# Expert matrices loaded as two halves with a semaphore each, and one transposed tile taken by ScalarE

## The chip, the core and the metric

The program runs on one core of one Trainium2 chip. Such a core has a matrix engine (TensorE, PE in the profile), a vector engine (DVE), an activation engine (ScalarE, ACT), GpSimd (POOL), a queue engine that issues transfers (SyncE, SP), and 16 DMA engines that share each transfer. The metric is the time of one execution on the device, in microseconds (us). A transfer is told to be complete by a semaphore that an engine waits on.

## The reference, cut to what matters

One layer over 256 tokens of width 1024, in float32. Three branches (chunked attention, a Mamba-2 scan, attention into a memory) are merged and added to x; then comes a mixture of experts, which the change is about:

```python
logits = (xt @ w_router + b_router)
top_val, top_idx = lax.top_k(logits, 4)          # 4 of 32 experts for each token
wts = softmax(top_val)
# for each expert e, its tokens' rows xblk:
g = xblk @ w_gate[e] + b_gate[e]                 # 1024 x 1024, float32: 4 MB
u = xblk @ w_up[e] + b_up[e]                     # 4 MB
g, u = min(g, 7.0), clip(u, -7.0, 7.0)
yb = ((u + 1) * g * sigmoid(1.702 * g)) @ w_down[e] + b_down[e]    # 4 MB
# weighted sum of yb over each token's experts, added to x
```

All 32 experts are computed, so 96 matrices of 4 MB are read from HBM.

## The kernel before, in words

The first part (up to about 520 us) streams the other weights through four buffers and computes the branches and the output projection. Its last block is the second column block of `w_out` (block "wo", 1), computed for two tiles of 128 tokens. For each tile t VectorE adds the product to x (`add_out`), TensorE turns (transposes) the upper four column chunks of the tile (`turn_out`), VectorE copies the turned columns out of PSUM into `xT` (`take_xT`, L1433), and TensorE finishes the router's logits from them (`last_logits`, L1618 is the router's matmul). Beside it ScalarE squares the tile with an accumulated sum (L899), VectorE scales the sum (`norm_begin`, L1439), ScalarE takes a root (L694), VectorE makes the inverse root and the top-4 choice (`choose`), and ScalarE writes the normed tile `h2` (L905).

The second part works through the 32 experts in order. For each expert TensorE does, in this order: the gate matmuls (`gate_or_up`, L1954), the scatter of the expert before (L1935), the up matmuls (L1954), the gather for the next expert (L1878) around the transposes of the activation, and the down matmuls (`down`, L1992). Each of the three matrices takes 8 chunks of 128 rows, two matmuls of 512 columns each; between chunk 3 and 4 of gate and up stand two matmuls of the bias (L1962).

The matrices are numbered m = 3e + k (k is 0 for gate, 1 for up, 2 for down) and go round five slots of 4 MB in the on-chip memory (slot m % 5). The SP queue issues the load of matrix m when matrix m - 5 is done with (semaphores `gate_done`, `up_done`, `down_done`). The loads of SP run in the order of issue. The first five matrices come in pieces during the first part. The loads m = 5 to 9 go out in two halves of 2 MB (chunks 0 to 3, then 4 to 7): the first half when TensorE has done the first half of matrix m - 5 (`half_done`), the second when it has done all of it. From m = 10 to 92 (83 matrices) one load brings the whole matrix in 32 KB runs, one for each of 128 partitions (L610), and TensorE waits for all of it before its first chunk. The last three matrices go out as two halves one behind the other, when the slot is free, with a semaphore for each half.

The experts 0 and 1 stand before TensorE's loop, 2 to 26 in a loop of five rounds of five, 27 to 31 behind it; SP's loop covers the loads m = 10 to 84.

Of the kernel before, what the change touches and what calls it, by code (L numbers as in the profile page):

```python
# [249 lines left out]
def hybrid_block_kernel(nc, x, mem, g_mix, w_in, w_dt, a_gains, rel_rev, conv_w, conv_b, dt_bias, a_log, d_skip,  # L250
                        g_ssm, g_mem, w_mem_kv, x_gains, w_br_a, w_br_b, w_br_c, w_out, norm_ffn, w_router,
                        b_router, w_gate, b_gate, w_up, b_up, w_down, b_down, bias_dram, out):
    with ExitStack() as ctx:
# [186 lines left out]
        MATRICES = EXPERTS * LOADS  # L440
        ROUND, ROUNDS = 5, 5
        AHEAD, TURNS = 2, ROUND * LOADS // SLOTS
        HALVED = MATRICES - LOADS
        FIRST_PIECES = (2, 2, 4, 4, 3)
        e_landed = [sem(f"expert_landed{k}") for k in range(SLOTS)]
        e_done = [sem("gate_done"), sem("up_done"), sem("down_done")]
        half_landed = [[sem(f"last_landed{k}{h}") for h in range(2)] for k in range(LOADS)]

        def landings(slot, turn):

            return 16 * (FIRST_PIECES[slot] + (turn and turn + 1))

        MISC_END = MISC_AT["end"]
        COUNT_BANK = EXP_BANK
# [48 lines left out]
        def _(sp):  # L503
# [8 lines left out]
                sp.dma_start(halves[:, m % HALVES], weight_src(name, i)[:, 4 * (m % 2):4 * (m % 2) + 4])\  # L512
                    .then_inc(landed[m % HALVES], 16)

            def matrix_load(m, c0=0, c1=KC, signal=None):

                slot, chunks = m % SLOTS, slice(c0, c1)
                sp.dma_start(eslots[slot][:, chunks], expert_src(m % LOADS, m // LOADS)[:, chunks])\
                    .then_inc(signal or e_landed[slot], 16)

            def bias_loads():

# [72 lines left out]
            sp.wait_ge(sem("x_opened"), 2 * TT)  # L595
            matrix_load(4, 6, 8)

            for m in range(SLOTS, 2 * SLOTS):
                freed = m - SLOTS
                sp.wait_ge(sem("half_done"), freed + 1)  # L600
                matrix_load(m, 0, 4)
                sp.wait_ge(e_done[freed % LOADS], freed // LOADS + 1)
                matrix_load(m, 4, 8)

            def round_loads(j, n0, n1):

                for n in range(n0, n1):
                    m, freed = 2 * SLOTS + n, SLOTS + n
                    sp.wait_ge(e_done[freed % LOADS], j * ROUND + freed // LOADS + 1)
                    sp.dma_start(eslots[m % SLOTS], expert_src(m % LOADS, j * ROUND + m // LOADS))\  # L610
                        .then_inc(e_landed[m % SLOTS], 16)

            with sp.Fori(0, ROUNDS) as j:
                round_loads(j, 0, ROUND * LOADS)
            round_loads(ROUNDS, 0, HALVED - 2 * SLOTS - ROUNDS * ROUND * LOADS)
            for k in range(LOADS):
                m = HALVED + k
                sp.wait_ge(e_done[(m - SLOTS) % LOADS], (m - SLOTS) // LOADS + 1)
                for half in range(2):
                    matrix_load(m, 4 * half, 4 * half + 4, half_landed[k][half])  # L620

            sp.wait_ge(sem("passes_known"), 1)
            n_pass = sp.value_load(npass_i[0:1, 0:1], min_val=1, max_val=PASSES)
            with sp.If(n_pass > 1):
                with sp.Fori(1, n_pass) as b:
                    with sp.Fori(0, EXPERTS) as e:
                        for k in range(LOADS):

                            sp.wait_ge(sem("down_done"), b * EXPERTS + e)
                            sp.dma_start(eslots[k], expert_src(k, e)).then_inc(half_landed[k][0], 16)  # L630
            for t in range(TT):
                sp.wait_ge(sem("y_ready"), t + 1)
                sp.dma_start(out[0, t * P:(t + 1) * P, 0:NB], y_out[:, 2 * t]).then_inc(sem("y_stored"), 16)
# [54 lines left out]
        def _(act):  # L688
# [207 lines left out]
            for t in range(TT):  # L896
                act.wait_ge(gemm_taken, GEMM_AT[("wo", 1, t)] + 1)
                act.wait_ge(sem("out_squares"), TT + t)
                act.activation(tmp[:, t], x_sb[:, t, NB:2 * NB], ACT.Square, accum_out=ss_part[:, TT + t:TT + t + 1])\  # L899
                    .then_inc(sem("out_squares"), 1)  # L900
                root(1)
                act.wait_ge(sem("second_norm"), t + 1)
                for h in range(2):
                    cols = slice(h * NB, (h + 1) * NB)
                    act.activation(h2[:, t].rearrange("q (c p) -> q c p", c=KC)[:, :, 64 * h:64 * h + 64],  # L905
                                   x_sb[:, t, cols].rearrange("q (p c) -> q c p", c=KC), ACT.Copy, scale=rs_2[:, t:t + 1]).then_inc(sem("h2_ready"), 1)
# [29 lines left out]
        def _(dve):  # L936
# [493 lines left out]
            def take_xT(t):  # L1430
# [2 lines left out]
                dve.tensor_copy(xT[:, 4:8, t * P:(t + 1) * P], ps[:, b, :].rearrange("p (c t) -> p c t", c=4))\  # L1433
                    .then_inc(misc_taken, 1)

            def norm_begin(t):

                dve.wait_ge(sem("out_squares"), TT + t + 1)
                link(dve.tensor_tensor(ss_2[:, t:t + 1], ss_part[:, t:t + 1], ss_part[:, TT + t:TT + t + 1], ALU.add))  # L1439
                variance(rs_2[:, t:t + 1], ss_2[:, t:t + 1], D)  # L1440
# [47 lines left out]
                dve.tensor_copy(pick[0:96], picks[0:96, column(i)].to_broadcast([96, BLK])).then_inc(sem("pick_ready"), 1)  # L1488

            add_out(0)  # L1490
            take_xT(0)
            norm_begin(0)
            choose(0)
            add_out(1)
            take_xT(1)
            norm_begin(1)
            find_first(0)
            choose(1)
            dve.tensor_tensor(e4, mx8[:, :, 0:TOP_K], mx8[:, :, 0:1].to_broadcast([P, TT, TOP_K]), ALU.subtract)\
# [81 lines left out]
        def _(pe):  # L1581
# [362 lines left out]
            pe.wait_ge(sem("logits_taken"), TT)  # L1944
            pe.wait_ge(sem("passes_known"), 1)
            n_pass = pe.value_load(npass_i[0:1, 0:1], min_val=1, max_val=PASSES)
            def gate_or_up(i, k, pieces, halves_done=False):

                bank = (G_BANK, U_BANK)[k]
                for slot, c0, c1, landed_at, count in pieces:  # L1950
                    pe.wait_ge(landed_at, count)
                    for c in range(c0, c1):
                        for h in range(2):
                            last = pe.matmul(ps[64 * h:64 * h + 64, bank, :].rearrange("j (m q) -> j m q", q=4),  # L1954
                                             xgT[:, c], hidden_of(eslots[slot][:, c], h),
                                             start=c == 0, stop=c == KC - 1, skip_group_check=True)
                        if c == KC // 2 - 1:
                            if halves_done:
                                last.then_inc(sem("half_done"), 1)
                            pe.wait_ge(sem("pick_ready"), i + 1)  # L1960
                            for h in range(2):
                                pe.matmul(ps[64 * h:64 * h + 64, bank, :].rearrange("j (m q) -> j m q", q=4),  # L1962
                                          pick[0:96], hidden_of(bias_parts[0:96, k], h),
                                          start=False, stop=False, skip_group_check=True)
                last.then_inc(e_done[k], 1)
# [12 lines left out]
                    last = turn(ps[:, G_BANK, c * P:(c + 1) * P], act_sb[:, c * P:(c + 1) * P])  # L1978
                last.then_inc(sem("actT_out"), 1)

            def down(i, pieces, halves_done=False):

                pe.wait_ge(sem("actT_ready"), i + 1)
                pe.wait_ge(sem("scatter_ready"), i + 1)
# [3 lines left out]
                for slot, c0, c1, landed_at, count in pieces:  # L1988
                    pe.wait_ge(landed_at, count)
                    for c in range(c0, c1):  # L1990
                        for h in range(2):
                            last = pe.matmul(ps[64 * h:64 * h + 64, D_BANK, :], actT[:, c % 4, 64 * (c // 4):64 * (c // 4) + 64],  # L1992
                                             eslots[slot][:, c, h * NB:(h + 1) * NB],
                                             start=False, stop=c == KC - 1, skip_group_check=True)
                        if halves_done and c == KC // 2 - 1:
                            last.then_inc(sem("half_done"), 1)
                last.then_inc(e_done[2], 1)

# [3 lines left out]
                    pe.matmul(ps[:, X_BANK, c % KC * BLK:(c % KC + 1) * BLK], h2[:, 0, c % KC * P:(c % KC + 1) * P],  # L2002
                              hot[:, 0], start=True, stop=True, skip_group_check=True)

            def expert(i, loads, ahead=True, halves_done=(False, False, False)):

                pe.wait_ge(sem("xg_ready"), i + 1)
                gate_or_up(i, 0, loads[0], halves_done[0])
                scatter(i)
                turn_places(i)  # L2010
                gate_or_up(i, 1, loads[1], halves_done[1])
                if ahead:
                    pe.wait_ge(sem("hot_ready"), i * TT + 2 * TT)
                    gather(0, 1)
# [2 lines left out]
                else:  # L2017
                    keep_warm(KC)
                    turn_activation(i)
                    keep_warm(KC // 2)  # L2020
                down(i, loads[2], halves_done[2])

            def whole(m, j=0):

                slot, turn = m % SLOTS, m // SLOTS
                return [(slot, 0, KC, e_landed[slot], landings(slot, turn) + 16 * TURNS * j)]

            for e in range(AHEAD):
                expert(e, [whole(LOADS * e + k) for k in range(LOADS)],
                       halves_done=[LOADS * e + k < SLOTS for k in range(LOADS)])  # L2030
            with pe.Fori(0, ROUNDS) as j:
                for r in range(ROUND):
                    e = AHEAD + r
                    expert(j * ROUND + e, [whole(LOADS * e + k, j) for k in range(LOADS)])
            for e in range(AHEAD + ROUNDS * ROUND, EXPERTS - 1):
                expert(e, [whole(LOADS * e + k) for k in range(LOADS)])
            expert(EXPERTS - 1, [[((HALVED + k) % SLOTS, 4 * half, 4 * half + 4, half_landed[k][half], 16)
                                  for half in range(2)] for k in range(LOADS)], ahead=False)

            with pe.If(n_pass > 1):  # L2040
                with pe.Fori(1, n_pass) as b:
                    with pe.Fori(0, EXPERTS) as e:
                        i = b * EXPERTS + e
                        pe.wait_ge(sem("hot_ready"), i * TT + TT)
                        gather()
                        expert(i, [[(k, 0, KC, half_landed[k][0], ((b - 1) * EXPERTS + e + 2) * 16)] for k in range(LOADS)],
                               ahead=False)
            scatter(n_pass * EXPERTS, sem("sums_ready"))

# [39 lines left out]
```

## Time and profile before

| | us |
|---|---|
| median of 3 runs | 1448.0 (1447.46 to 1449.2) |
| the profiled execution | 1448.57 |
| its span, first to last instruction | 1446.5 |
| TensorE busy | 1425.7 (99%) |
| VectorE busy | 589.0 (41%) |
| ScalarE busy | 407.0 (28%) |

The granted clock of TensorE is 0.999 over the span. The page says that matmuls are pipelined and that their ends are modelled, so a high busy share is no proof that no other limit is near: the chain of waits and the DMA rows have to be read with it. The time between an issue of a transfer and its landing holds the waiting behind the transfers ahead of it in the queue.

### The profile page before, as it was taken

Reading aid. Unit: us, or ns where it says so; the run is one execution under the profiler, and the core shown is the slowest. Engines: PE = TensorE matmul, PEld = TensorE weight load, DVE = VectorE, ACT = ScalarE, POOL = GpSimd, SP = SyncE. Lnnn points to the kernel's source line nnn. Section 1 sums busy time; section 2 is a strip of 40 time slices with the busy share of each in tenths; the row PEclk is TensorE's granted clock in tenths of the full one; section 3 lists DMA queues with packets and bytes.
Section 4 is the critical chain, followed back from the end, with each engine's and each line's share of the span. In section 5 each row is a group of like instructions: output and inputs, shape, how many; then the busy total and the mean of one; then the engine's idle time right before and its main releaser. Section 6 shows DMA issues by size and latency. Waiting matters only on the chain.

```text
span 1446.5 us, 18510 instructions
## 1 busy us (share of the span) xinstructions
PE 1425.7 (99%) x7576; PEld 823.3 (57%) x7576; DVE 589.0 (41%) x1154; ACT 407.0 (28%) x605; POOL 63.9 (4%) x50
## 2 busy tenths in 40 slices
PE   7999999999999999999999999999999999999998
PEld 6998888777788864444444444444444444444433
DVE  6789788677788651211212121121212112111211
ACT  5766666556544531101010110101011010101100
POOL 5110000121100000000000000000000000000000
PEclk9999999999999999999999999999999999999999
DMA  7455544655563989999999999999999999999996
GB/s 237 157 190 173 162 136 160 197 162 164 171 244 139 382 328 420 406 432 434 433 425 433 433 435 431 426 435 433 434 428 430 433 435 432 428 432 433 432 424 255
DMA packets 62646, 490.84 MB, mean 339 GB/s; under 512 B 4009, under 2 KB 7729, under 8 KB 48001
## 3 DMA queue, kind: packets, MB, share of 16 engines
q1 hardware_dynamic: 59920, 487.04, 82.9%
q10 hardware_dynamic: 2160, 2.62, 0.6%
q8 instruction: 38, 0.62, 0.2%
q0 software_dynamic: 512, 0.43, 0.2%
q14 instruction: 16, 0.12, 0.0%
HBM read 488.41 MB, written 1.07 MB: 338 GB/s over the span
## 4 chain that ended last, share of the span: by engine, by line
PE 88%; DMA 6%; DVE 4%; ACT 1%; issue 1%; ACTq 0%; SPq 0%; DVEq 0%
PE ps L1954 29%; PE ps L1992 13%; PE ps L1611 8%; PE ps L1613 8%; PE ps L1612 8%; PE ps L1878 7%; DMA regions<-in_w_gate 6%; PE ps L1935 4%; PE ps L1598 4%; DVE regions L1187 1%; DVE splits L1041 1%; PE ps L1832 1%; PE ps L1962 1%; PE ps L1986 1%; ACT splits L726 0%
## 5 line engine op out<-in xcount | busy, mean ns | idle before, releaser
L1954 PE MATMUL ps<-regions,sig 128*64 128x512 f32 x2048 | 463.0, 594 | 3.8 <-DMA regions<-in_w_gate 3.6
L1954 PEld LDWEIGHTS ps<-regions,sig 128*64 128x64 f32 x2048 | 143.8, 137 | 274.1 <-issue 266.8
L1992 PE MATMUL ps<-regions,tmp 128*64 128x512 f32 x1024 | 225.1, 592 | 0.0
L1611 PE MATMUL ps<-splits,regions_r 128*128 128x512 f32 x512 | 205.7, 402 | 0.1
L1613 PE MATMUL ps<-splits,regions_r 128*128 128x512 f32 x512 | 200.1, 391 | 0.0
L1612 PE MATMUL ps<-splits,regions_r 128*128 128x512 f32 x512 | 199.8, 390 | 0.0
L726 ACT ACTIVATE splits<-halves 128x1024 fp32r<-128x1024 f32 x152 | 159.2, 1056 | 93.4 <-PE ps L1613 82.1
L1041 DVE TENSOR_TENSOR splits<-halves,splits 128x1024 fp32r<-128x1024 f32 x132 | 162.2, 1232 | 42.9 <-ACT splits L726 41.5
L914 ACT ACTIVATE work<-work 128x512 f32<-128x512 f32 x32 | 20.1, 629 | 473.9 <-DVE work L1545 473.9
L1992 PEld LDWEIGHTS ps<-regions,tmp 128*64 128x64 f32 x1024 | 71.5, 137 | 132.2 <-issue 129.8
L1878 PEld LDWEIGHTS ps<-craw,regions 128*128 128x128 f32 x1024 | 119.3, 192 | 25.6 <-issue 25.1
L1878 PE MATMUL ps<-craw,regions 128*128 128x64 f32 x1024 | 124.7, 275 | 0.4 <-DVE craw L1466 0.4
L1550 DVE TENSOR_SCALAR work<-ps 128x512 f32<-128x512 f32 x32 | 22.1, 691 | 238.8 <-PE ps L1954 238.8
L1611 PEld LDWEIGHTS ps<-splits,regions_r 128*128 128x128 f32 x512 | 96.2, 188 | 22.4 <-issue 3.9
L1559 DVE COPY sig<-ps 128x512 f32<-128x512 f32 x32 | 22.1, 691 | 211.1 <-PE ps L1992 211.1
L1613 PEld LDWEIGHTS ps<-splits,regions_r 128*128 128x128 f32 x512 | 96.1, 188 | 20.9
L1612 PEld LDWEIGHTS ps<-splits,regions_r 128*128 128x128 f32 x512 | 96.3, 188 | 18.6
L919 ACT ACTIVATE tmp<-ps 128x512 f32<-128x512 f32 x32 | 19.1, 597 | 302.1 <-PE ps L1598 302.1
L1545 DVE TENSOR_SCALAR work<-ps 128x512 f32<-128x512 f32 x32 | 22.1, 692 | 177.0 <-PE ps L1954 177.0
L1935 PE MATMUL ps<-sig,craw 64*128 64x512 f32 x264 | 65.6, 615 | 0.8 <-DVE sig L1559 0.8
L681 POOL TENSOR_TENSOR splits<-halves,splits 128x1024 fp32r<-128x1024 f32 x20 | 49.8, 2491 | 327.9 <-ACT splits L726 327.9
L1611 PE MATMUL ps<-regions_r,splits 128*128 128x256 f32 x192 | 55.5, 289 | 0.0
(304 smaller groups left out, 1192.2 us busy)
## 6 DMA issues: line engine op xcount, KB each, us to landing
regions<-in_w_up SPq DMA_DIRECT2D x28, 4096.0 KB, 27.2
regions<-in_w_down SPq DMA_DIRECT2D x28, 4096.0 KB, 29.8
regions<-in_w_gate SPq DMA_DIRECT2D x27, 4096.0 KB, 29.4
halves<-in_w_in SPq DMA_DIRECT2D x48, 1024.0 KB, 5.1
regions<-in_w_gate SPq DMA_DIRECT2D x8, 2048.0 KB, 11.4
regions<-in_w_up SPq DMA_DIRECT2D x7, 2048.0 KB, 11.9
regions<-in_w_down SPq DMA_DIRECT2D x6, 2048.0 KB, 12.3
halves<-in_w_br_b SPq DMA_DIRECT2D x8, 1024.0 KB, 5.1
```

Source lines behind the costliest of these rows:

```text
L681: pool.tensor_tensor(lo, raw, hi.bitcast(F32), ALU.subtract).then_inc(lo_ready_pool, 1)
L726: act.activation(hi, raw, ACT.Copy).then_inc(hi_ready, 1)
L1041: dve.tensor_tensor(lo, raw, hi.bitcast(F32), ALU.subtract).then_inc(lo_ready, 1)
L1545: dve.tensor_scalar(g_sb, ps[:, G_BANK, :], LIMIT, None, ALU.min).then_inc(sem("g_ready"), 1)
L1598: return pe.transpose(dst, src, ident[:])
L1611: pe.matmul(out, lhs[0], rhs[0], start=start, stop=False, skip_group_check=True)
L1612: pe.matmul(out, lhs[1], rhs[0], start=False, stop=False, skip_group_check=True)
L1613: return pe.matmul(out, lhs[0], rhs[1], start=False, stop=stop, skip_group_check=True)
L1878: last = pe.matmul(ps[:, X_BANK, c * BLK:(c + 1) * BLK], h2[:, t, c * P:(c + 1) * P], hot[:, t], start=(t == 0 and c == 0), stop=(t == TT ...
L1935: last = pe.matmul(ps[:, ACC[2 * t + h], :], hot_wT[rows, t], yb[rows], start=False, stop=False, skip_group_check=True)
L1954: last = pe.matmul(ps[64 * h:64 * h + 64, bank, :].rearrange("j (m q) -> j m q", q=4), xgT[:, c], hidden_of(eslots[slot][:, c], h), start= ...
L1992: last = pe.matmul(ps[64 * h:64 * h + 64, D_BANK, :], actT[:, c % 4, 64 * (c // 4):64 * (c // 4) + 64], eslots[slot][:, c, h * NB:(h + 1) ...
```

## The change

Three things change in the code. First, every load from m = 5 on goes out as two halves of 2 MB in 16 KB runs, the first half when the first half of matrix m - 5 is done with, the second when all of it is; this is now so inside SP's loop too, which therefore starts at m = 5. Second, each slot has two semaphores, one for each half, and TensorE waits for a half ahead of that half's chunks, in every matrix; it signals `half_done` in every matrix. Third, the turned columns of the second tile are copied out of PSUM by ScalarE, right behind its squares, and VectorE waits at that place for it (`left_to_scalar`); on VectorE `norm_begin(0)` now stands ahead of `take_xT(0)`.

```diff
-        FIRST_PIECES = (2, 2, 4, 4, 3)
-        e_landed = [sem(f"expert_landed{k}") for k in range(SLOTS)]
+        FIRST_PIECES = ((1, 1), (1, 1), (2, 2), (2, 2), (1, 2))
+        e_landed = [[sem(f"expert_landed{k}{h}") for h in range(2)] for k in range(SLOTS)]
...
-            for m in range(SLOTS, 2 * SLOTS):
+            def reload(m, j=0):
+
                 freed = m - SLOTS
-                sp.wait_ge(sem("half_done"), freed + 1)
-                matrix_load(m, 0, 4)
-                sp.wait_ge(e_done[freed % LOADS], freed // LOADS + 1)
-                matrix_load(m, 4, 8)
-
-            def round_loads(j, n0, n1):
-
-                for n in range(n0, n1):
-                    m, freed = 2 * SLOTS + n, SLOTS + n
-                    sp.wait_ge(e_done[freed % LOADS], j * ROUND + freed // LOADS + 1)
-                    sp.dma_start(eslots[m % SLOTS], expert_src(m % LOADS, j * ROUND + m // LOADS))\
-                        .then_inc(e_landed[m % SLOTS], 16)
+                sp.wait_ge(sem("half_done"), j * ROUND * LOADS + freed + 1)
+                matrix_load(m, 0, 4, j * ROUND)
+                sp.wait_ge(e_done[freed % LOADS], j * ROUND + freed // LOADS + 1)
+                matrix_load(m, 4, 8, j * ROUND)
 
             with sp.Fori(0, ROUNDS) as j:
-                round_loads(j, 0, ROUND * LOADS)
-            round_loads(ROUNDS, 0, HALVED - 2 * SLOTS - ROUNDS * ROUND * LOADS)
-            for k in range(LOADS):
-                m = HALVED + k
-                sp.wait_ge(e_done[(m - SLOTS) % LOADS], (m - SLOTS) // LOADS + 1)
-                for half in range(2):
-                    matrix_load(m, 4 * half, 4 * half + 4, half_landed[k][half])
+                for m in range(SLOTS, SLOTS + ROUND * LOADS):
+                    reload(m, j)
+            for m in range(SLOTS + ROUNDS * ROUND * LOADS, MATRICES):
+                reload(m)
...
+                if t == 1:
+                    n_misc = MISC_AT["tail"] + t
+                    act.wait_ge(misc_ready, n_misc + 1)
+                    act.activation(xT[:, 4:8, t * P:(t + 1) * P],
+                                   ps[:, MISC_BANKS[n_misc % 3], :].rearrange("p (c t) -> p c t", c=4), ACT.Copy)\
+                        .then_inc(misc_taken, 1)
...
             add_out(0)
+            norm_begin(0)
             take_xT(0)
-            norm_begin(0)
             choose(0)
             add_out(1)
-            take_xT(1)
             norm_begin(1)
+            left_to_scalar()
...
-                            if halves_done:
-                                last.then_inc(sem("half_done"), 1)
+                            last.then_inc(sem("half_done"), 1)
...
-            def whole(m, j=0):
+            def in_halves(m, j=0):
 
                 slot, turn = m % SLOTS, m // SLOTS
-                return [(slot, 0, KC, e_landed[slot], landings(slot, turn) + 16 * TURNS * j)]
+                return [(slot, 4 * half, 4 * half + 4, e_landed[slot][half], landings(slot, half, turn) + 16 * TURNS * j)
+                        for half in range(2)]
```

On SP's queue, where the reloads of the slots end their straight part and enter the loop, there stood before the halves of m = 8 and 9, the loop's head and its first whole loads (128 partitions of 8192 elements are a whole matrix, 4096 are a half):

```order
44 L518 DMA regions<-in_w_down 128x4096 x2
45 L518 DMA regions<-in_w_gate 128x4096 x2
46 L613 UNCONDITIONAL_BRANCH
47 L613 ISA
48 L610 ISA
49 L610 DMA regions<-in_w_up 128x8192
50 L610 DMA regions<-in_w_down 128x8192
```

At the end of the loop and behind it there stands now, on the same queue:

```order
89 L517 DMA regions<-in_w_up 128x4096 x2
90 L605 REGISTER_ALU
91 L605 COMPARE_AND_BRANCH
92 L517 DMA regions<-in_w_down 128x4096 x2
93 L517 DMA regions<-in_w_gate 128x4096 x2
94 L517 DMA regions<-in_w_up 128x4096 x2
```

Every whole load has become two halves; the order of the matrices is as it was.

On VectorE, at the second tile of the last output block, there stood before (`regions<-ps 128x4x128` is the copy of the turned columns):

```order
585 L1427 TENSOR_TENSOR regions<-regions,ps 128x512
586 L1433 COPY regions<-ps 128x4x128
587 L1439 TENSOR_TENSOR stat<-stat 128x1
588 L957 TENSOR_SCALAR stat<-stat 128x1
589 L1464 TENSOR_TENSOR rt<-ps,chosen_r 128x32
```

On ScalarE the same stretch now reads (the squares of the second tile, then the copy, the root, and the two halves of `h2`):

```order
292 L888 ACTIVATE tmp,stat<-regions 128x512
293 L893 ACTIVATE regions<-ps 128x4x128
294 L683 ACTIVATE stat<-stat 128x1
295 L900 ACTIVATE regions<-regions,stat 128x8x64 x2
```

The copy of the second tile has moved from VectorE to ScalarE, ahead of the root.

## Rows read from the trace of the kernel before

**Rows 1.** The page: span, TensorE's busy time, DMA share in 40 slices.

```profile
span 1446.5 us, 18510 instructions
PE 1425.7 (99%) x7576; PEld 823.3 (57%) x7576; DVE 589.0 (41%) x1154; ACT 407.0 (28%) x605; POOL 63.9 (4%) x50
DMA  7455544655563989999999999999999999999996
```

**Rows 2.** Waits of TensorE: in total us, times, longest us.

```profile
PE ps L1954 <- DMA regions<-in_w_gate: 3.6, 3, 2.2
```

**Rows 3.** Chain that ended last: start us, us, what; expert 1.

```profile
563.03 3.43 PE ps L1954 x16
...
584.30 6.87 PE ps L1992 x32
591.17 3.43 PE ps L1954 x16
```

**Rows 4.** The same chain, from the loop's end to the last expert's end.

```profile
1283.20 40.54 DMA regions<-in_w_gate
...
1340.85 42.65 DMA regions<-in_w_gate
1383.50 0.14 issue
1383.63 3.65 PE ps L1954 x16
...
1412.07 3.43 PE ps L1954 x16
...
1428.71 1.93 PE ps L2002 x16
...
1432.45 6.90 PE ps L1992 x32
```

**Rows 5.** DMA queue: packets, MB, share of 16 engines; 1000:1300, then 1403:1427.

```profile
q1 hardware_dynamic: 4449, 129.53, 100.3%
...
q1 hardware_dynamic: 708, 10.29, 100.8%
```

**Rows 6.** Timeline of SP's queue: start us, us, instruction; five issues.

```profile
563.07 0.33 SPq L518 DMA_DIRECT2D regions<-in_w_up  x1
...
579.70 0.33 SPq L518 DMA_DIRECT2D regions<-in_w_gate  x1
...
692.40 0.33 SPq L610 DMA_DIRECT2D regions<-in_w_gate  x1
...
1369.98 0.80 SPq L518 DMA_DIRECT2D regions<-in_w_gate  x2
...
1390.99 0.80 SPq L518 DMA_DIRECT2D regions<-in_w_down  x2
```

**Rows 7.** First load of each of rows 6: KB, us from issue to landing.

```profile
regions<-in_w_up SPq DMA_DIRECT2D x1, 2048.0 KB, 10.2
...
regions<-in_w_gate SPq DMA_DIRECT2D x1, 2048.0 KB, 13.2
...
regions<-in_w_gate SPq DMA_DIRECT2D x1, 4096.0 KB, 19.3
...
regions<-in_w_gate SPq DMA_DIRECT2D x1, 2048.0 KB, 37.8
...
regions<-in_w_down SPq DMA_DIRECT2D x1, 2048.0 KB, 36.4
```

**Rows 8.** Timeline around the second tile's copy, with idle time and releaser.

```profile
525.76 0.63 ACT L899 ACTIVATE tmp<-regions 128x512 f32<-128x512 f32 x1 [1.45 <-DVE regions L1427]
...
526.30 0.19 ACT L899 ACTIVATION_READ_ACCUMULATOR tmp<-regions 128x1 f32 x1
...
526.37 1.10 PE L1885 MATMUL ps<-regions,ident 128*128 128x512 f32 x2
526.54 0.69 DVE L1433 COPY regions<-ps 128x512 f32<-128x512 f32 x1 [0.81 <-PE ps L1905]
...
527.31 0.50 PE L1618 MATMUL ps<-wr_sb,regions 128*128 128x32 f32 x3
```

**Rows 9.** The page's groups: a ScalarE copy of 512 columns out of PSUM.

```profile
L919 ACT ACTIVATE tmp<-ps 128x512 f32<-128x512 f32 x32 | 19.1, 597 | 302.1 <-PE ps L1598 302.1
```

More of the change, by code:

```diff
@@ L442, in hybrid_block_kernel, with landings @@
         AHEAD, TURNS = 2, ROUND * LOADS // SLOTS
-        HALVED = MATRICES - LOADS
-        FIRST_PIECES = (2, 2, 4, 4, 3)
-        e_landed = [sem(f"expert_landed{k}") for k in range(SLOTS)]
+        FIRST_PIECES = ((1, 1), (1, 1), (2, 2), (2, 2), (1, 2))
+        e_landed = [[sem(f"expert_landed{k}{h}") for h in range(2)] for k in range(SLOTS)]
         e_done = [sem("gate_done"), sem("up_done"), sem("down_done")]
-        half_landed = [[sem(f"last_landed{k}{h}") for h in range(2)] for k in range(LOADS)]
-        def landings(slot, turn):
-            return 16 * (FIRST_PIECES[slot] + (turn and turn + 1))
+        again_landed = [sem(f"again_landed{k}") for k in range(LOADS)]
+        def landings(slot, half, turn):
+            return 16 * (FIRST_PIECES[slot][half] + turn)
         MISC_END = MISC_AT["end"]
@@ L513, in load, with matrix_load @@
                     .then_inc(landed[m % HALVES], 16)
-            def matrix_load(m, c0=0, c1=KC, signal=None):
+            def matrix_load(m, c0, c1, before=0):
                 slot, chunks = m % SLOTS, slice(c0, c1)
-                sp.dma_start(eslots[slot][:, chunks], expert_src(m % LOADS, m // LOADS)[:, chunks])\
-                    .then_inc(signal or e_landed[slot], 16)
+                sp.dma_start(eslots[slot][:, chunks], expert_src(m % LOADS, before + m // LOADS)[:, chunks])\
+                    .then_inc(e_landed[slot][c0 // 4], 16)
             def bias_loads():
@@ L629, in _ @@
                             sp.wait_ge(sem("down_done"), b * EXPERTS + e)
-                            sp.dma_start(eslots[k], expert_src(k, e)).then_inc(half_landed[k][0], 16)
+                            sp.dma_start(eslots[k], expert_src(k, e)).then_inc(again_landed[k], 16)
             for t in range(TT):
@@ L1434, in take_xT, with left_to_scalar @@
                     .then_inc(misc_taken, 1)
+            def left_to_scalar():
+                misc[0] += 1
+                dve.wait_ge(misc_taken, misc[0])
             def norm_begin(t):
@@ L1946, in _, with gate_or_up @@
             n_pass = pe.value_load(npass_i[0:1, 0:1], min_val=1, max_val=PASSES)
-            def gate_or_up(i, k, pieces, halves_done=False):
+            def gate_or_up(i, k, pieces):
                 bank = (G_BANK, U_BANK)[k]
@@ L1979, in turn_activation, with down @@
                 last.then_inc(sem("actT_out"), 1)
-            def down(i, pieces, halves_done=False):
+            def down(i, pieces):
                 pe.wait_ge(sem("actT_ready"), i + 1)
@@ L1994, in down @@
                                              start=False, stop=c == KC - 1, skip_group_check=True)
-                        if halves_done and c == KC // 2 - 1:
+                        if c == KC // 2 - 1:
                             last.then_inc(sem("half_done"), 1)
@@ L2003, in keep_warm, with expert @@
                               hot[:, 0], start=True, stop=True, skip_group_check=True)
-            def expert(i, loads, ahead=True, halves_done=(False, False, False)):
+            def expert(i, loads, ahead=True):
                 pe.wait_ge(sem("xg_ready"), i + 1)
-                gate_or_up(i, 0, loads[0], halves_done[0])
+                gate_or_up(i, 0, loads[0])
                 scatter(i)
                 turn_places(i)
-                gate_or_up(i, 1, loads[1], halves_done[1])
+                gate_or_up(i, 1, loads[1])
                 if ahead:
@@ L2020, in expert @@
                     keep_warm(KC // 2)
-                down(i, loads[2], halves_done[2])
-            def whole(m, j=0):
+                down(i, loads[2])
+            def in_halves(m, j=0):
                 slot, turn = m % SLOTS, m // SLOTS
-                return [(slot, 0, KC, e_landed[slot], landings(slot, turn) + 16 * TURNS * j)]
+                return [(slot, 4 * half, 4 * half + 4, e_landed[slot][half], landings(slot, half, turn) + 16 * TURNS * j)
+                        for half in range(2)]
             for e in range(AHEAD):
-                expert(e, [whole(LOADS * e + k) for k in range(LOADS)],
-                       halves_done=[LOADS * e + k < SLOTS for k in range(LOADS)])
+                expert(e, [in_halves(LOADS * e + k) for k in range(LOADS)])
             with pe.Fori(0, ROUNDS) as j:
@@ L2033, in _ @@
                     e = AHEAD + r
[L2034 to L2038, printed above, removed]
+                    expert(j * ROUND + e, [in_halves(LOADS * e + k, j) for k in range(LOADS)])
+            for e in range(AHEAD + ROUNDS * ROUND, EXPERTS):
+                expert(e, [in_halves(LOADS * e + k) for k in range(LOADS)], ahead=e < EXPERTS - 1)
             with pe.If(n_pass > 1):
@@ L2045, in _ @@
                         gather()
-                        expert(i, [[(k, 0, KC, half_landed[k][0], ((b - 1) * EXPERTS + e + 2) * 16)] for k in range(LOADS)],
+                        expert(i, [[(k, 0, KC, again_landed[k], ((b - 1) * EXPERTS + e + 1) * 16)] for k in range(LOADS)],
                                ahead=False)
```

## The prediction, made before the changed kernel ran

> **What bounds the kernel now.** I read the page's busy shares and 40 slices first. TensorE is busy 99% of the span, and from the sixteenth slice on the DMA engines are at nine tenths or more as well [rows 1]. Two resources are thus near their limit in the expert stage, and the page alone doesn't say which one ends it. The waits of TensorE name only 3.6 us in three waits, all for a gate matrix [rows 2]. The chain of waits shows how the two compare: in expert 1 it is TensorE alone, 591.17 - 563.03 = 28.14 us for three matrices [rows 3]. Late in the stage it runs over two DMA pieces, of 40.54 and 42.65 us from issue to landing, and TensorE starts 0.14 us after the second has landed [rows 4]. In the middle of the stage such a load took 19.3 us [rows 6, 7]. So the time to landing grows while TensorE goes on undisturbed: the DMA engines are a little slower than TensorE and use up a lead.
>
> Their rate comes from landings a known number of matrices apart. The gate load issued at 692.40 landed at 711.70 [rows 6, 7], the one issued at 1283.20 at 1323.74 [rows 4]; 21 experts, 63 matrices, lie between them, so a whole matrix takes 612.04 / 63 = 9.715 us, 29.14 for an expert against TensorE's 28.14. That is 1.0 us of lead lost in each expert. The lead is gone near the end of the loop; from there the DMA engines set the pace. From 1323.74 to the landing at 1383.50 (1340.85 + 42.65) six matrices took 59.76 us where 6 x 9.715 = 58.3 were due: 1.5 us were lost once, just behind the place where the loops end [rows 4]. The cause isn't in these rows.
>
> **The change, part by part.** *Loads in halves.* What a free slot half gives is an earlier issue, and what a landed half gives is an earlier start. The second counts only where TensorE waits, the first only where the DMA engines would run dry. They are busy 100.3% of the time from 1000 to 1300 [rows 5], and a load lands 19.3 us after its issue at 692 and 40.5 at 1283 [rows 4, 6, 7], so loads are always queued and an earlier issue moves nothing through them faster. The number of bytes is the same. What is left is the price of a transfer in halves.
>
> That price can be read, because the kernel before has halves in two places. Second halves of m = 7 and 9, issued at 563.07 and 579.70, landed at 573.27 and 592.90: two matrices in 19.63 us, 9.815 each. First halves of m = 93 and 95, issued at 1369.98 and 1390.99, landed at 1407.78 and 1427.39: 19.61, 9.805 each [rows 6, 7]. The places are far apart, one with 10 us of loads queued and one with 37, and agree. I take 9.81, and a matrix in halves costs 9.81 - 9.715 = 0.095 us more. The rounding of the landings (0.1 us) leaves 0.05 to 0.14. A second reading goes by the busy time of the engines for each MB: 1.003 x 300 / 129.53 = 2.323 us from 1000 to 1300, all in whole matrices, and 1.008 x 24 / 10.29 = 2.351 from 1403 to 1427, all in halves [rows 5]: 1.2%, or 0.118 us for 4.19 MB. So 83 matrices change from whole to halves at 0.05 to 0.14 us: 4 to 12 us of DMA time, 8 by my value.
>
> *The sum.* The DMA queue is full from the load that lands at 592.90 on: the first half of m = 10 now goes out near 584.30 + 3.43 = 587.7 [rows 3], before that landing. The second half of the last up matrix, m = 94, is 85 matrices later: 592.90 + 85 x 9.81 = 1426.75. Behind it TensorE has, from rows of the last experts, 0.14 to start [rows 4], 3.65 for the second half of up, as in the half-matrix behind a wait [rows 4], 1432.45 - 1428.71 = 3.74 for the turned activation and bias, and 6.90 for down: 14.43, an end at 1441.18. The other chain through the last expert (its gate's first half lands three halves earlier, then gate, scatter and up without a pause) comes to the same within 0.1. The last down half lands two halves, 9.81 us, after m = 94 and has 0.8 us to spare for its own 3.4 us of matmuls.
>
> To this I add the 1.5 us lost behind the loops. Both loops end at nearly the same place in both programs and with the same kind of code behind them, so I take it to come again: 1442.7. Before, the last down matmul ended at 1432.45 + 6.90 = 1439.35 [rows 4]. The difference is +3.3 us.
>
> Check of the wait that goes: the 3.6 us of waits [rows 2] are what the DMA pace costs before. They don't vanish, they grow, and are spread over halves: small waits at the gate's first and second half of each expert, from about expert 26 on, some 1.2 us for each.
>
> *Signals and waits on TensorE.* Some 90 more signals and as many more waits. Expert 1 has its gate and up signalled by halves and took 28.14 us [rows 3]; in the last expert, whose matrices are waited for by halves, half a gate takes 3.43 us at 1412.07 as it does at 591.17 in the loop [rows 3, 4]. I take 0. From above, 90 waits at the 0.14 us that a start takes behind a wait would be 12 us, but that is paid only where the semaphore isn't there yet. From below it is 0, since nothing is removed.
>
> *SP's queue.* Twice the issues at 0.33 us [rows 6], 6 for an expert of 28 us, with nothing behind them but loads in the same order. A half waits for TensorE's own half, so the queue never stands in its own way. 0.
>
> *The second tile's copy.* VectorE copied the turned columns at 526.54 in 0.69 us, and TensorE's router matmuls, which need them, start at 527.31; TensorE is still in the matmuls of L1885 until 526.37 + 1.10 = 527.47 [rows 8]. ScalarE has done with its squares at 526.30 + 0.19 = 526.49 [rows 8], so it is free at the same moment, and such a copy takes it 0.60 us [rows 9]. So the router starts within 0.1 us of where it did. What VectorE wins (0.69 us off its queue) falls in a stretch where TensorE works on without a wait for it. If ScalarE's copy comes late by d, the router's matmuls come late by d less 0.1: I bound it by -0.2 and +0.3 and take 0. `norm_begin(0)` ahead of the first copy puts two small instructions into time in which VectorE waits for the turned columns: 0.
>
> The sum is +3.3 us. The profiled execution took 1448.57 us, 2.1 over its span and 0.6 over the median of 1448.0. From the median: 1448.0 + 3.3 = 1451.3.
>
> **A rule that speaks against it.** The landings above say that a matrix in two transfers costs 0.095 us more [rows 6, 7]. The Trainium skill, page "DMA: Bandwidth & Descriptors", section "Anatomy of one DMA", says that on trn2 the semaphore write's bubble is about one cycle, essentially free, and its "Rules for kernel authors" ask only for 1 MiB per transfer, which halves of 2 MB meet. By that rule splitting is free, and the first rival below would be the outcome.
>
> **The rivals.** *A: halves cost nothing, faster.* If the two places with halves are slow for a reason of their own (both stand in straight code outside the loops, not in the stretch where whole loads were timed), the rate stays 9.715. Then m = 94 lands at 592.90 + 85 x 9.715 = 1418.7, with the 1.5 us 1420.2, and the end by the same 14.43 is 1434.6. TensorE alone, 30 periods of 28.14 from 563.03 and then the 27.28 us that the last expert takes (1439.35 - 1412.07 [rows 4]), gives 1434.5. So -4.8 us, 1443.2. It decides from a price below 0.055 us for a matrix, where the end is the old one; at 0.04 the end would be 1438.0. For it speaks that no row shows halves inside the loop; against it, that two places 830 us apart agree to 0.01 us, and that the busy time for each MB says the same.
>
> *B: the 1.5 us don't come again.* The sum is then +1.8 us, 1449.8. For it speaks that it is seen once only. Against it, that it follows the loops' end, which stays.
>
> *C: halves are dearer, or a second such loss comes.* At 0.118 us for a matrix, by the busy time, the sum gains 85 x 0.023 = 2.0 us: +5.3, 1453.3. A second loss of 1.5 us gives 1452.8.
>
> *D: the change isn't felt.* If TensorE alone set the pace, nothing but the 3.6 us of waits could change. The growth from 19 to 42 us to landing speaks against it.
>
> **How the numbers follow.** About 0.2%, 2.9 us, is what can be told from no change here. Forecast (+3.3): 0.45; B: 0.2; C: 0.15; A: 0.2. Of the forecast a third of its weight lies below 2.9 us by the rounding of the price, say 0.1 of 0.45. Slower: 0.35 + 0.15 = 0.50. Same: 0.10 + 0.20 = 0.30. Faster: 0.20, all of A. The range takes in B and C with the upper end of the copy's bound, and of A the part with a small price: 1444.0 to 1453.5. The forecast's own range is 1449.5 to 1453.
>
> **What would show it.** Landings of matrices one expert apart in the loop: 29.4 us, not 29.1. DMA packets of 16 KB throughout, and a busy time of 2.35 us for each MB. Time to landing of a half near 40 us at the end, and waits of TensorE for gate (and a little for up) of 6 to 9 us in total, from about expert 26 on. No change of the 28.14 us of an expert before that, and the first matmul of expert 0 within 0.3 us of where it was. I am wrong if the loop shows 29.14 us for three matrices in halves (A), or if an expert takes TensorE more than 28.2 us without a wait for DMA.

## The result, and the profile after

| | median us | runs |
|---|---|---|
| before | 1448.13 (1447.3 to 1449.95) | 22 |
| changed | 1450.11 (1448.86 to 1451.31) | 22 |

The ratio is 1.0013, with a 95% interval of 1.0007 to 1.0019: the change makes the kernel 2.0 us slower. The profiled execution has a span of 1448.1 us against 1446.5, 1.6 more, so the difference can be followed in the two traces. The page after, in the lines that answer to [rows 1]:

```profile
span 1448.1 us, 18768 instructions
PE 1426.6 (99%) x7576; PEld 821.8 (57%) x7576; DVE 588.6 (41%) x1153; ACT 407.5 (28%) x606; POOL 63.9 (4%) x50
DMA  7455545655464989999999999999999999999996
```

At this grain nothing has moved. The waits of TensorE have (in total us, times, longest), against [rows 2]:

```profile
PE ps L1954 <- DMA regions<-in_w_gate: 4.2, 6, 0.9
...
PE ps L1954 <- DMA regions<-in_w_up: 0.4, 1, 0.4
```

There are more of them and each is shorter: before, three waits with one of 2.2 us, now seven of at most 0.9. They begin earlier too. The chain that ended last (start us, us, what) goes over its first DMA piece one expert sooner than in [rows 4], and then over one for every second expert:

```profile
1254.50 43.37 DMA regions<-in_w_gate
...
1311.39 46.41 DMA regions<-in_w_gate
...
1371.33 45.56 DMA regions<-in_w_gate
...
1426.71 3.65 PE ps L1954 x16
1430.37 1.93 PE ps L2001 x16
...
1434.11 6.90 PE ps L1991 x32
```

The last rows are the ones that the forecast's sum was built of: the second half of the last up matrix, the turning of the activation, and down. TensorE's last down matmul ends at 1434.11 + 6.90 = 1441.01, against 1439.35 before.

The price of halves inside the loop can now be read. In SP's timeline (start us, us, instruction) a second half of a gate matrix goes out at 691.96, and its row of DMA issues says 18.6 us to landing:

```profile
691.96 0.33 SPq L517 DMA_DIRECT2D regions<-in_w_gate  x1
```

```profile
regions<-in_w_gate SPq DMA_DIRECT2D x1, 2048.0 KB, 18.6
```

It landed at 710.56, and the one issued at 1254.50 at 1297.87. They are 20 experts apart: 587.31 / 60 = 9.79 us for a matrix, against 9.715 before. The DMA queue's row (packets, MB, share of 16 engines) from 1000 to 1300, which answers to the first of [rows 5], says the same: 128.54 MB where before 129.53 went through, 0.76% less.

```profile
q1 hardware_dynamic: 8821, 128.54, 100.6%
```

The packets have doubled (4449 before). The second tile's copy, against [rows 8]:

```profile
525.91 0.18 ACT L888 ACTIVATION_READ_ACCUMULATOR tmp<-regions 128x1 f32 x1
525.98 1.10 PE L1885 MATMUL ps<-regions,ident 128*128 128x512 f32 x2
...
526.15 0.60 ACT L893 ACTIVATE regions<-ps 128x512 f32<-128x512 f32 x1
...
526.92 0.97 PE L1618 MATMUL ps<-wr_sb,regions 128*128 128x32 f32 x8
```

The router's matmuls start 526.92 - 525.98 = 0.94 us behind L1885, before 527.31 - 526.37 = 0.94. ScalarE's copy is done at 526.75 and TensorE doesn't feel the difference.

### The profile page after: what moved, and what is told of

Read it like the earlier page. It is cut to its first block, busy times and chain, and to the rows that moved or that the text cites. A ratio compares the mean times of both kernels' runs of the same rounds, so it can differ in the third digit from the quotient of the medians.

```text
span 1448.1 us, 18768 instructions
## 1 busy us (share of the span) xinstructions
PE 1426.6 (99%) x7576; PEld 821.8 (57%) x7576; DVE 588.6 (41%) x1153; ACT 407.5 (28%) x606; POOL 63.9 (4%) x50
## 3 DMA queue, kind: packets, MB, share of 16 engines
HBM read 488.41 MB, written 1.07 MB: 338 GB/s over the span
## 4 chain that ended last, share of the span: by engine, by line
PE 84%; DMA 10%; DVE 4%; ACT 1%; issue 1%; ACTq 0%; DVEq 0%
PE ps L1954 27%; PE ps L1991 12%; DMA regions<-in_w_gate 9%; PE ps L1611 8%; PE ps L1613 8%; PE ps L1612 8%; PE ps L1878 7%; PE ps L1935 4%; PE ps L1598 4%; DVE regions L1182 1%; DVE splits L1036 1%; PE ps L1832 1%; PE ps L1961 1%; PE ps L1985 1%; ACT splits L715 0%
```

## The experiments

Times are medians, with the ratio to the kernel before, run on the same chip, and its 95% interval. "Lost time" below is how much longer the landings took from the first half of m = 7 to the last up half, m = 94, than 9.715 us for each whole matrix and 4.895 for each half make.

**Which part carries the difference: `copy_only` and `halves_only`.** The first is the kernel before with the ScalarE and VectorE edits alone:

```diff
+                if t == 1:
+                    act.wait_ge(misc_ready, n_misc + 1)
+                    act.activation(xT[:, 4:8, t * P:(t + 1) * P], ...).then_inc(misc_taken, 1)
...
-            take_xT(1)
+            left_to_scalar()
```

> The kernel before with only the second tile's copy on ScalarE and norm_begin(0) ahead of the first copy; the loads are as before. My theory: nothing on the path, 0.0 to -0.2 us against before (from the traces, 9.73 us from the first open_sum to expert 0's first matmul before, 9.63 in the changed kernel). Rival (ScalarE's copy comes late and holds the router's matmuls): slower by 0.3 us or more.

Measured: 1448.00 against 1448.03, ratio 0.9997 (0.9988 to 1.0006). The second is the changed kernel without those edits.

> The changed kernel with the second tile's copy and norm_begin put back on VectorE as before; all loads in halves. My theory: the loads carry the whole difference, +1.5 to +2.3 us against before, landings of halves 4.895 us apart in the loop. Rival (the copy's move costs and the halves do not): within 0.5 us of before.

Measured: 1450.29, ratio 1.0016 (1.0007 to 1.0025), +2.3 us. The loads carry the whole difference.

**What is dear in a half: `one_load_short_runs` and `quarters`.** Halves differ from whole loads in two ways: twice the transfers with a completion each, and runs of 16 KB instead of 32. The first kernel changes the runs alone:

```diff
-                    sp.dma_start(eslots[m % SLOTS], expert_src(m % LOADS, j * ROUND + m // LOADS))\
+                    sp.dma_start(halves_swapped(eslots[m % SLOTS]),
+                                 expert_src(m % LOADS, j * ROUND + m // LOADS).rearrange("p (h c) n -> p h (c n)", h=2))\
```

> The kernel before, but each whole load in the loops is still one transfer with one completion, now in 16 KB runs instead of 32 KB (the first and second 16 KB of each partition land in swapped places, so that the products pair wrong rows; the work is the same). Theory R (the price is one for each run): landings 9.79 us apart, last landing 83 x 0.075 = 6.2 us later, time +3.5 to +4.5 us. Theory P (the price is one for each transfer and its completion): landings 9.715 us apart as before, time within 0.3 us of before.

Measured: 1454.40, ratio 1.0041 (1.0026 to 1.0057). The landings in the loop are 9.79 us apart (the slope over 58 landings), just as in the changed kernel, with one transfer for each matrix. So the price is one for the shorter runs, and a second transfer with its completion costs nothing that these traces show. The time is 6.4 us longer and not the 3.5 to 4.5 expected: TensorE here waits for whole matrices at the lower rate. The last DMA piece of its chain is a whole up matrix of the last expert but one, which lands at 1399.97, and TensorE works on from there without a wait to its last down matmul:

```profile
1358.62 41.35 DMA regions<-in_w_up
```

The second kernel cuts each half once more:

```diff
+                for c in range(c0, c1, 2):
+                    chunks = slice(c, c + 2)
+                    sp.dma_start(eslots[slot][:, chunks], ...).then_inc(e_landed[slot][c0 // 4], 16)
```

> The changed kernel with each half load split once more, into two transfers of 1 MB in 8 KB runs; waits and places in the order as in the changed kernel. If the price is a constant for each further piece (0.075 us for the second), four pieces cost 3 x 0.075 = 0.225 us: 9.94 us for a matrix, last landing 85 x 0.15 = 12.8 us later than in the changed kernel, time +14 to +15 us against before. Rival (the DMA engines have the same rate for any piece of 1 MB or more, and the 9.79 us of the changed kernel have another cause such as the issue in halves): the time of the changed kernel, +2 us.

Measured: 1463.65, ratio 1.0113 (1.0098 to 1.0129), +16.1 us, 1.1 above the expected range; the last up piece lands 13.1 us later than in the changed kernel, where 12.8 were expected. The queue's rows from 1000 to 1200 of this kernel, then of `one_load_short_runs`, then of the changed one:

```profile
q1 hardware_dynamic: 11587, 84.37, 101.3%
```

```profile
q1 hardware_dynamic: 5552, 85.66, 100.6%
```

```profile
q1 hardware_dynamic: 5888, 85.72, 100.7%
```

4.194 MB x 200 / 84.37 = 9.94 us for a matrix in quarters, as expected, and 9.79 for both others. The last two rows also show the completions apart from the runs: for a matrix `one_load_short_runs` has 5552 x 4.194 / 85.66 = 272 packets (256 runs and 16 more), the changed kernel 288 (256 and 32), at the same rate. Each of the 16 engines moves 8 runs of a whole matrix, 16 of one in 16 KB runs, 32 of one in 8 KB runs: (9.79 - 9.715) / 8 and (9.94 - 9.715) / 24 are both 9 ns for each run more.

**A cut by partitions: `two_loads_long_runs`.**

```diff
+                    for q in range(2):
+                        lanes = slice(64 * q, 64 * q + 64)
+                        sp.dma_start(eslots[m % SLOTS][lanes], expert_src(...)[lanes])\
+                            .then_inc(e_landed[m % SLOTS], 16)
```

> The kernel before, but each whole load in the loops goes out as two transfers of 64 partitions each, in 32 KB runs, TensorE still waits for both. Theory P (a price for each transfer): two transfers 9.79 us for a matrix, time +3.5 to +4.5 us. Theory R (a price for each run): 9.715 us for a matrix and the time of before within 0.3 us. If 64 partitions at a time use the engines or ports unevenly, both are wrong and the matrix takes clearly over 9.8 us.

Measured: 2299.87, ratio 1.5892 (1.5868 to 1.5916). Both theories' numbers are missed, and the reserve that the expectation named holds, far more than "clearly". Its queue from 1000 to 1200:

```profile
q1 hardware_dynamic: 1602, 42.01, 100.2%
```

The engines are as busy as ever and move 210 GB/s, half of the usual rate. Why 64 partitions at a time are so slow is not shown here. So this kernel doesn't tell a price for a transfer from one for a run; `one_load_short_runs` does.

**What the start by halves is worth: `wait_for_both`.** The changed kernel with both waits ahead of the first chunk:

```diff
-                for slot, c0, c1, landed_at, count in pieces:
-                    pe.wait_ge(landed_at, count)
+                for piece in pieces:
+                    pe.wait_ge(*piece[3:5])
+                for slot, c0, c1, landed_at, count in pieces:
```

> The changed kernel, but TensorE waits for both halves ahead of the first chunk of each matrix; loads, their order and issue as in the changed kernel. My theory: the same landings; the start by halves is worth half a matrix at the last waits, 3.6 us: time +5 to +6 us against before. Rival (the DMA pace alone sets the end, and the start by halves is worth nothing): +2 us as the changed kernel.

Measured: 1453.88, ratio 1.0043 (1.0028 to 1.0058), +6.4 us, 4.4 more than the changed kernel and 0.4 above the expected range. The end of its chain:

```profile
1387.01 40.01 DMA regions<-in_w_up
1427.02 0.14 issue
1427.16 3.65 PE ps L1955 x16
...
1431.04 3.44 PE ps L1955 x16
```

The last up half lands at 1427.02, within 0.4 us of where it does in the changed kernel (1426.64 by its issue and time to landing), and now all of the up matrix stands behind it, not half. The halves' semaphores are thus worth half a matrix and a little: with the shorter runs and waits for whole matrices the kernel is 6.4 us slower, the waits by halves give back 4.4, and 2.0 are left. That `one_load_short_runs` comes to 6.4 as well is partly luck: there the last up half lands 2.3 us later (1429.36), but the last expert is still waited for by halves.

**Halves only where TensorE waits: `late_halves` and `mostly_whole`.** The first is the kernel before with halves from m = 85 on instead of 93; of its edit, the line that sets this:

```diff
-        HALVED = MATRICES - LOADS
+        HALVED = 2 * SLOTS + ROUNDS * ROUND * LOADS
```

> The kernel before with whole loads up to m = 84 and halves with a semaphore each from m = 85 (before: from m = 93); issue of both halves when the slot is free. My theory: 8 matrices more at 0.075 us cost 0.6 us, the start by halves gives back the waits for whole loads: the end is set by the landing of the last up half, 14.4 us ahead of it, 1437.6 against 1439.4 before: -1.5 to -2 us. Rival (halves cost their price and give nothing): +0.6 us.

Measured: 1445.73 against 1447.52, ratio 0.9987 (0.9978 to 0.9997), -1.8 us. The end of the chain:

```profile
1368.18 43.96 DMA regions<-in_w_gate
...
1421.98 3.65 PE ps L1953 x16
...
1429.38 6.90 PE ps L1991 x32
```

The last down matmul ends at 1436.28. Landings are at the pace of before, and the end follows the last up half as in the changed kernel.

The second adds an early issue for m = 10 and the move of the copy; of its edit, the lines for m = 10:

```diff
-            for m in range(SLOTS, 2 * SLOTS):
+            for m in range(SLOTS, EARLY):            # EARLY = 2 * SLOTS + 1
```

> As late_halves, with m = 10 too in halves with an early issue, the loop of whole loads over m = 11 to 85, halves from m = 86, and the second tile's copy on ScalarE. My theory: the DMA engines no longer run dry at about 592 us (2.2 us in the trace of before), so the landings come 2 us earlier: 592.9 + 9.79 + 75 x 9.715 + 9 x 9.79 + 1.5 = 1420.9, + 14.4 = 1435.3 against 1439.35: -3.5 to -4.5 us against before, and TensorE alone is nearly the limit. Rival (the gap at 592 us is made up for by nothing, since the loss has another cause): -1.5 to -2 us as late_halves.

Measured: 1445.29, ratio 0.9981 (0.9972 to 0.9990), -2.2 us. This beats both the kernel before and the changed one; from `late_halves` it can't be told, since the two intervals overlap. My theory of it is wrong by half. The gap near 592 us did go: the load of m = 11 lands at 597.24 + 14.5 = 611.74, before at 598.32 + 16.2 = 614.52. But of the 2.3 us lost there before, only 1.0 us stands at m = 10, where the queue ran short; 1.3 us stand at m = 11. And in `mostly_whole` landings are 0.6, 1.5 and 1.4 us late at 631.8, 662.3 and 1412.4 us, so that the lost time is 3.6 us in this kernel as in the one before (2.9 in `late_halves`). The rival's number held. What the late landings are is the next question.

**What the lost time is: `straight_15` and `straight_25`.** A landing that is late by 1.35 us stands behind the loops in the changed kernel as well (the rows of issue at 1294.13 and 1297.57, landings 42.9 and 45.7 us later). Around it the DMA queue's rows (1340 to 1342) show a packet of instructions:

```profile
q1 hardware_dynamic: 56, 0.79, 92.3%
q8 instruction: 1, 0.02, 3.4%
```

In the traces of the kernel before and of the changed one such packets come until about 726 us, the end of the loop's first round, and again from 1312 on. To test the link I gave the same work more code outside the loops:

```diff
-        ROUND, ROUNDS = 5, 5
+        ROUND, ROUNDS = 5, 3        # straight_25: 5, 1
```

> The changed kernel with three rounds of the loops instead of five: experts 17 to 31 stand as straight code behind the loop (15 instead of 5), the work and its order are the same. Theory F (the landings lost behind the loops come from fetching instructions, since the 16 KB packets of the instruction queue stop at about 726 us and start again at 1312 us in the traces): these packets now begin near 1030 us, some 11 more of them ahead of the last landings, and the lost time, 3.4 us in the changed kernel from the landing of m = 7 to that of m = 94, grows by 2 to 4 us; time +2 to +4 us against the changed kernel, so +4 to +6 against before. Rival (the losses have nothing to do with the code): the time of the changed kernel, +2 us against before.

> The changed kernel with one round of the loops: experts 7 to 31 stand as straight code. Theory F: some 22 more instruction packets than in the changed kernel, from about 730 us on without a pause, lost time up by 4 to 8 us, time +6 to +10 us against before. Rival: +2 us as the changed kernel, and no growth from 15 to 25 straight experts.

Measured: 1451.65, ratio 1.0028 (1.0017 to 1.0040), and 1454.15, ratio 1.0044 (1.0027 to 1.0061): +3.6 and +6.1 us. The instruction queue's row from 568 to 1420 in the changed kernel, in `straight_15` and in `straight_25`:

```profile
q8 instruction: 12, 0.20, 0.1%
```

```profile
q8 instruction: 23, 0.38, 0.2%
```

```profile
q8 instruction: 35, 0.57, 0.3%
```

The time grows with the packets: both medians lie above the changed kernel's, by 1.6 and 4.1 us, though `straight_15` is just below the +4 us expected and its interval touches the changed kernel's. The lost time is 3.4, 4.3 and 6.0 us, a growth of 0.9 and 2.6 where 2 to 4 and 4 to 8 were expected. One trace of each is a weak measure of it: among the kernels with the changed kernel's packets it goes from 1.7 us (`wait_for_both`) to 4.2 (`one_load_short_runs`). Only `straight_25` stands clear of that.

Stronger evidence lies in where the late landings are. In `straight_25` they come at every eighth packet, and add up to the whole lost time (all in us):

| packet starts | next late landing | late by | next packet starts | next late landing | late by |
|---|---|---|---|---|---|
| 699.6 | 705.3 | 0.46 | 726.4 | 730.8 | 1.07 |
| 895.2 | 897.8 | 0.45 | 922.6 | 928.2 | 1.09 |
| 1091.2 | 1095.1 | 0.46 | 1112.5 | 1115.7 | 1.04 |
| 1286.1 | 1292.4 | 0.46 | 1311.6 | 1317.9 | 1.10 |

The other traces have the same period. Counted from the packet at about 558 us, the landings late by over 1 us stand behind packets 3, 11 and 19 in `straight_15`, behind 2 and 10 in the changed kernel, behind 3 and 11 in the kernel before (apart from the 1.0 us at m = 10), and behind 8 alone in `wait_for_both`, which therefore lost so little. A packet itself takes about as long as such a landing is late; the row of `straight_25` from 1112 to 1113, 6.8% of 16 engines' 1 us, is 1.09 us:

```profile
q8 instruction: 1, 0.02, 6.8%
```

So the instruction packets go with the late landings, but only one to three in eight cost anything. That would fit packets that go over eight engines in turn, of which a few have no time to spare; which engine took a packet, and why the place in the eight differs between kernels, is not shown.

## Why the prediction was right, and where its size was off

The sign, the mechanism and the place are as forecast: the halves' lower rate makes the last up matrix land later, and the end follows it. The forecast was +3.3 us, the runs gave +2.0 and the trace +1.66 (1441.01 against 1439.35). The measured 1450.1 lies in the forecast's own range, 1449.5 to 1453. By the 2.9 us that the prediction took as the least that can be told from no change, though, the result is no change, to which it gave 0.30 against 0.50 for slower. The interval of 22 runs each, about 1.0 to 2.8 us, does tell it from nothing.

In the traces the last up half lands 4.2 us later (1426.7 against 1422.5), and TensorE ends 14.3 us behind it where it was 16.8 before, since before it waited for whole matrices. The 4.2 us are 83 x 0.075 = 6.2 from the rate, less 0.24 from an earlier start, less 1.8 because less time was lost behind 592.9 us than before (there 3.7). Of these 1.8 us, 1.0 is the gap at m = 10 that the early issue closes. The prediction called an earlier issue worth nothing, but its sum holds this gain, as it counts from 592.90 with a full queue. The other 0.8 is how the late landings happened to fall.

By the sum's own steps:

- *The rate of halves* was the mis-sized term. I took 9.81 us for a matrix; it is 9.79. Over 85 matrices that is 1.7 us too much, nearly the whole error. The two places it was read from are two matrices long each, and the times to landing are rounded to 0.1 us, which is up to 0.05 for a matrix. The landings at hundredths (573.32 and 592.86, 1407.81 and 1427.38) give 9.77 and 9.78; that rounding raised both places alike, so that they seemed to confirm each other, was luck. The busy time for each MB, which seemed to confirm and even to raise it, is a worse measure still: it grew by 1.1% in the loop (1.006 x 300 / 128.54 = 2.348 against 2.323) where the rate fell by 0.76%.
- *The start of the count* was 0.24 us earlier (592.66), from a difference already there in the first part, ahead of the tail.
- *The loss behind the loops*: 1.8 us were lost after 592.66 where 1.5 was taken, 1.5 of them behind the loops and the rest at 632 us. It was put down to the loops' end without a cause. The packets of straight code go with it, by the rows of `straight_25`. That it fell at the same place again is partly luck: in `wait_for_both`, with the same loads, 1.3 us were lost at 731.7 us and 0.3 behind the loops.
- *The end behind the last up half*: 1441.01 - 1426.64 = 14.37, taken 14.43.
- Together: 1442.7 - 1.7 - 0.24 + 0.33 - 0.06 = 1441.0.
- *Signals and waits on TensorE, SP's queue, the copy*: all taken at 0. `copy_only` shows the copy within 0.1% of it. An expert in the loop still takes 28.13 to 28.16 us until the first wait.
- *The waits of TensorE* were forecast at 6 to 9 us and are 4.6, in keeping with the smaller price.
- *Rival A*, halves at no cost, had 0.2. It is out: 9.79 us in the loop, in the changed kernel, `halves_only` and `wait_for_both`. *B* falls with the loss that came again, though its number, 1449.8, is nearer to the measured 1450.1 than the forecast's 1451.3; that is luck, since the mis-sized rate was as large as the loss. *C* falls with the price below my own, *D* with the waits.

The rule that was weighed came out half right. `one_load_short_runs` has one completion for each matrix and the same 9.79 us, so the trace agrees with the Trainium skill, page "DMA: Bandwidth & Descriptors", section "Anatomy of one DMA": a completion's semaphore write costs next to nothing on trn2. (The section is on transfers issued by GpSimd; those here are issued by SyncE.) What didn't follow from it is that halves are free, because a half of this matrix also has runs half as long. The same page's section "Why small descriptors are slow" speaks of a fixed overhead for each packet, with a 256-byte example; here 9 ns for each run show from 8 to 32 KB, in a queue that is never empty.

## What to carry to other kernels

Where transfers use up a lead over hundreds of microseconds, their rate to a per cent is worth more than where they wait or when they are issued: compare landings dozens of transfers apart, not neighbours. One trace can hold a microsecond or two of loss that the next, with the same loads, does not. Cut a load only where its consumer waits for it (here the last ten or eleven matrices), and keep the longest contiguous runs everywhere else. A cut that looks like finer waiting also changes the runs, and the two are to be priced apart.

## What the runs showed of the hardware that was not expected

- A transfer to 64 partitions at a time ran at 210 GB/s with the engines' busy share at 100%, against 432 for 128 partitions. So the share of busy time does not tell the rate. The granted clock of TensorE was 0.835 over the span of that kernel, in which it was busy 70%.
- A matrix takes 9 ns more for each further run on an engine, the same from 32 to 16 and from 16 to 8 KB.
- Code that runs once costs DMA time beside it: with 23 further packets of 16 KB in a saturated queue `straight_25` took 4.1 us longer than the changed kernel and lost 2.6 us more in its landings, about three times what the packets' bytes (0.57 - 0.20 = 0.37 MB) take at its rate of 428 GB/s, 0.9 us. Two packets in eight went with all of its late landings, 0.46 and 1.07 us each, and the other six with none.
